# A fused fp32 transformer chain on one core: the two x halves of the FFN gate and up products in one 512-column matmul

## The reference, cut to what matters

```python
def swiglu(h, w_gate, w_up, w_down):                 # layers 0 and 1
    return (jax.nn.silu(h @ w_gate) * (h @ w_up)) @ w_down

def conv_ffn(x, g, w_up, dw_w, dw_b, w_down):        # layer 2
    h = causal_depthwise_conv(rms_norm_2(x, g) @ w_up, dw_w, dw_b)   # 3 taps over the tokens
    gate, up = h[..., :D_FF_2], h[..., D_FF_2:]
    return (jax.nn.silu(gate) * up) @ w_down
```

## Time and profile before

| | |
|---|---|
| time before, median of 3 runs | 981.87 us (979.51 to 983.39) |
| the profiled execution's own time | 980.03 us |
| its span (first to last instruction) | 978.3 us |
| PE busy | 934.4 us, 96% |
| PEld busy | 852.5 us, 87% |
| DVE busy | 535.2 us, 55% |
| ACT busy | 475.8 us, 49% |
| POOL busy | 336.8 us, 34% |
| mean granted TensorE clock | 0.984 of full |

### The profile page before, as it was taken

One profiled execution on the slowest core, in us unless ns is written; L12 is line 12 of the kernel. 1 busy time (PEld: TensorE's weight loads), 2 busy tenths in 40 slices (PEclk: granted clock), 3 DMA queues, 4 the chain that ended last, 5 costly groups with the idle time before them and its releaser, 6 DMA issues.

```text
span 978.3 us, 16764 instructions
## 1 busy us (share of the span) xinstructions
PE 934.4 (96%) x6404; PEld 852.5 (87%) x6404; DVE 535.2 (55%) x882; ACT 475.8 (49%) x767; POOL 336.8 (34%) x188
## 2 busy tenths in 40 slices
PE   4999999999999999999999999898999989999996
PEld 4899999999977899999999999586798789999995
DVE  3874444335455574444445595665565575666655
ACT  4753444434554574344444442467444465555542
POOL 1364433340000064444333279700100154444441
PEclk9999999999999999999999999798999999999999
DMA  9686666532431767666644665201443476566601
GB/s 302 199 251 200 193 193 188 179 116 80 160 117 45 213 200 235 178 186 193 193 151 130 174 155 185 87 1 44 130 172 86 151 222 192 178 182 193 193 22 44
DMA packets 187406, 154.35 MB, mean 158 GB/s; under 512 B 6573, under 2 KB 172685, under 8 KB 187357
## 3 DMA queue, kind: packets, MB, share of 16 engines
q1 hardware_dynamic: 184941, 148.67, 49.9%
q0 software_dynamic: 752, 2.39, 1.0%
q10 hardware_dynamic: 1664, 2.60, 0.8%
HBM read 152.04 MB, written 1.05 MB: 156 GB/s over the span
## 4 chain that ended last, share of the span: by engine, by line
PE 86%; DVE 5%; ACT 4%; POOL 2%; issue 1%; DMA 1%; SPq 0%; DVEq 0%; ACTq 0%
PE bank L1620 25%; PE bank L1622 25%; PE bank L1621 25%; PE bank L1712 2%; DMA raw<-in_pool_w 1%; DVE wl L964 1%; PE bank L2038 1%; PE bank L1637 1%; ACT wh L555 1%; PE bank L2110 1%; PE bank L1932 1%; PE bank L2187 1%; POOL st L1511 1%; PE bank L1931 1%; PE bank L2166 1%
## 5 line engine op out<-in xcount | busy, mean ns | idle before, releaser
L1531 POOL TENSOR_TENSOR dl<-draw,dh 128x1024 fp32r<-128x1024 f32 x66 | 239.4, 3630 | 292.8 <-ACT dh L599 292.7
L1620 PE MATMUL bank<-xh,wh 128*128 128x256 f32 x1192 | 338.8, 284 | 1.3 <-DVE xl L1182 0.7
L1622 PE MATMUL bank<-xh,wl 128*128 128x256 f32 x1192 | 338.1, 284 | 0.0
L1621 PE MATMUL bank<-xl,wh 128*128 128x256 f32 x1192 | 338.0, 284 | 0.0
L1620 PEld LDWEIGHTS bank<-xh,wh 128*128 128x128 f32 x1192 | 228.2, 191 | 5.4 <-DVE wl L964 1.2
L1621 PEld LDWEIGHTS bank<-xl,wh 128*128 128x128 f32 x1192 | 228.1, 191 | 3.0
L1622 PEld LDWEIGHTS bank<-xh,wl 128*128 128x128 f32 x1192 | 228.3, 192 | 0.3
L964 DVE TENSOR_TENSOR wl<-raw,wh 128x2048 fp32r<-128x2048 f32 (+5 forms) x53 | 112.5, 2129 | 57.6 <-ACT wh L555 57.6
L1064 DVE TENSOR_TENSOR wl<-raw,wh 128x2048 fp32r<-128x2048 f32 x57 | 137.4, 2410 | 1.4 <-ACT wh L622 1.4
L622 ACT ACTIVATE wh<-raw 128x2048 fp32r<-128x2048 f32 x57 | 108.7, 1906 | 6.4 <-DMA raw<-in_ffn_w_up 6.4
L1620 PE MATMUL bank<-dh,hh 128*128 128x512 f32 x264 | 105.1, 398 | 3.3 <-DVE hl L1070 3.3
(11 more groups left out here) (299 smaller groups left out, 1439.0 us busy)
## 6 DMA issues: line engine op xcount, KB each, us to landing
raw<-in_ffn_w_up SPq DMA_DIRECT2D x88, 512.0 KB, 6.1
draw<-in_ffn_w_down SPq DMA_DIRECT2D x66, 512.0 KB, 3.5
raw<-in_ffn_w_gate SPq DMA_DIRECT2D x44, 512.0 KB, 5.3
raw<-in_w_in SPq DMA_DIRECT2D x18, 512.0 KB, 5.1
raw<-in_xattn_wk SPq DMA_DIRECT2D x8, 512.0 KB, 4.6
raw<-in_mla_w_o SPq DMA_DIRECT2D x8, 512.0 KB, 4.0
raw<-in_xattn_wv SPq DMA_DIRECT2D x8, 512.0 KB, 4.3
raw<-in_w_out SPq DMA_DIRECT2D x8, 512.0 KB, 4.4
```

What stands on the lines that cost most here:

```text
L1531: pool.tensor_tensor(dl[s][:, :], draw[s][:, :], dh[s][:, :].bitcast(F32), ALU.subtract) \
L1620: pe.matmul(outp, a_hi, b_hi, start=start, stop=False, **kw)
L1621: pe.matmul(outp, a_hi, b_lo, start=False, stop=False, **kw)
L1622: return pe.matmul(outp, a_lo, b_hi, start=False, stop=stop, **kw)
```

## The change

**PE.** `xh` and `xl` become the two halves of one tile `xhl`. In `up`, each weight slice is used by one 512-column matmul, wh x (xh, xl), whose two 256-column results go to the left and right half of a bank, and by one 256-column matmul, wl x xh, which is added to the left half. Gate has a bank of its own, up another; even steps use banks 4 and 5, odd ones 6 and 7. The semaphore `gate_done` tells when the gate half of a step is done, `block_used` the end of the step, as before. `first_up` does step 0 in the old 256-column products, into the new places.

**DVE.** The two halves of a bank are added by a `tensor_reduce` of two elements, 512 values in and 256 out, to a tile in SBUF: `gs` for the gate, `us` for up. The low part of a slice (`weights_before`, slice j + 2) is made between the two additions, no longer at the end of the step before. All that follows (in ffn2 the taps) reads `gs` and `us` in SBUF instead of the bank.

**ACT.** Tanh (or the start of the gate's convolution) waits for `gs` only; `cu` waits for `us`. In ffn2 the tanh now stands ahead of the copy to `wh`. Loops have six steps instead of three. SP and POOL have no line changed.

The diff, without the lines that only rename or count:

```diff
-        xh = sb("xh", [P, KD, SEQ], F32R)
-        xl = sb("xl", [P, KD, SEQ], F32R)
+        xhl = sb("xhl", [P, 2, KD, SEQ], F32R)
+        xh, xl = xhl[:, 0, :, :], xhl[:, 1, :, :]
...
+        gs = at_("gs", [P, SEQ])
+        us = at_("us", [P, SEQ])
... ACT, step
+                    act.wait_ge(gate_sum, m + 1)
+                    if layer < 2:
+                        act.activation(th[s][:, :], gs[:, :], ACT.Tanh, scale=0.5).then_inc(tanh_done, 1)
+                    else:
+                        conv_start(0, gs, cg[s])
+                        act.wait_ge(up_sum, m + 1)
+                        conv_start(1, us, cu[s])
+                        act.wait_ge(conv_tap, 4 * (j + 1) - 2)
+                        act.activation(th[s][:, :], cg[s][:, :], ACT.Tanh, scale=0.5).then_inc(tanh_done, 1)
                     act.wait_ge(block_used, n + 1)
... DVE, step
+                    dve.wait_ge(gate_done, m + 1)
+                    dve.tensor_reduce(gs[:, :], pair[0][:, :].rearrange("p (a s) -> p s a", a=2), AX.X, ALU.add) \
+                       .then_inc(gate_sum, 1)
+                    if jj > 0:
+                        weights_before(j, i, jj)
+                    dve.wait_ge(gate_sum, m + 1)
+                    dve.wait_ge(block_used, n + 1)
+                    dve.tensor_reduce(us[:, :], pair[1][:, :].rearrange("p (a s) -> p s a", a=2), AX.X, ALU.add) \
+                       .then_inc(up_sum, 1)
+                    dve.wait_ge(up_sum, m + 1)
+                    g, u = gs[:, :], us[:, :]
                     if layer == 2:
+                        taps(0, gs, cg[s])
+                        taps(1, us, cu[s])
...
+                def weights_before(j, i, jj):
+                    if i is not None or jj + 2 < STEPS:
+                        ns = (n0 + jj - 1) % 3
+                        dve.wait_ge(hi_done, n0 + j + 3)
+                        dve.tensor_tensor(wl[ns][:, :], raw[ns][:, :], wh[ns][:, :].bitcast(F32),
+                                          ALU.subtract).then_inc(lo_done, 1)
+                    else:
+                        lo(n0 + jj + 2)
... PE, up
                     for half in range(2):
+                        b = bank[4 + 2 * (jj % 2) + half]
                         for k in range(KD):
                             a = (2 * k + half) * P
-                            ins = three(bank[4 + s][:, half * SEQ:(half + 1) * SEQ], wh[ns][:, a:a + P],
-                                        wl[ns][:, a:a + P], xh[:, k, :], xl[:, k, :], k == 0, k == KD - 1)
-                    ins.then_inc(block_used, 1)
+                            pe.matmul(b[:, :].rearrange("p (a s) -> p a s", a=2), wh[ns][:, a:a + P], xhl[:, :, k, :],
+                                      start=k == 0, stop=False, skip_group_check=True)
+                            ins = pe.matmul(b[:, 0:SEQ], wl[ns][:, a:a + P], xh[:, k, :], start=False,
+                                            stop=k == KD - 1, skip_group_check=True)
+                        ins.then_inc((gate_done, block_used)[half], 1)
```

More of the change, by code:

```diff
@@ L647, in ffn @@
                 step(0, None, 0)
-                with act.Fori(0, LOOPED // 3) as i:
-                    for s in range(1, 4):
-                        step(3 * i + s, i, s)
+                with act.Fori(0, LOOPED // 6) as i:
+                    for s in range(1, 7):
+                        step(6 * i + s, i, s)
                 for j in range(LOOPED + 1, STEPS):
@@ L1036, in step @@
                     n, m = n0 + j, m0 + j
-                    g, u = bank[4 + s][:, 0:SEQ], bank[4 + s][:, SEQ:2 * SEQ]
-                    if layer == 2:
[L1040 to L1049, removed]
+                    pair = bank[4 + 2 * (jj % 2)], bank[5 + 2 * (jj % 2)]
@@ new lines, in taps @@
+                    def taps(half, src, dst):
+                        dve.wait_ge(conv_in, 2 * j + half + 1)
+                        for back in (1, 2):
+                            if back == 2:
+                                dve.wait_ge(conv_tap, 4 * j + 2 * half + 1)
+                            c = C_DW + (2 - back) * NF2 + half * STEPS
+                            dve.scalar_tensor_tensor(
+                                out=dst[:, back:SEQ], in0=src[:, 0:SEQ - back],
+                                scalar=col[:, bass.ds(j + c, 1)], in1=dst[:, back:SEQ],
+                                op0=ALU.mult, op1=ALU.add).then_inc(conv_tap, 1)
@@ L1058, in step @@
                                              op0=ALU.mult, op1=ALU.mult).then_inc(prod_done, 1)
[L1060 to L1067, removed]
                     dve.wait_ge(h_hi, m + 1)
@@ L1073, in step @@
                         after(before)
-                    next_weights()
+                def weights_before(j, i, jj):
[6 more added lines that the diff above has]
+                        lo(n0 + jj + 2)
                 step(0, None, 0)
-                with dve.Fori(0, LOOPED // 3) as i:
-                    for s in range(1, 4):
-                        step(3 * i + s, i, s)
+                with dve.Fori(0, LOOPED // 6) as i:
+                    for s in range(1, 7):
+                        step(6 * i + s, i, s)
                 for j in range(LOOPED + 1, STEPS):
                     step(j, None, j)
+                lo(n0 + STEPS + 2)
             def after(name):
                 lo(at[name] + 3)
-            dve.sem_inc(prod_done, 3)
+            dve.sem_inc(prod_done, 2)
             dve.wait_ge(pos_loaded, 16)
@@ L1719, in ffn, with first_up @@
                     pe.wait_ge(cols_done, 2)
+                pe.wait_ge(mem_out, (1, 4, 8)[layer])
+                def first_up():
+                    pe.wait_ge(lo_done, n0 + 1)
+                    for of_lo in (False, True):
+                        for k in range(KD):
+                            pe.wait_ge(t_lo if of_lo else t_hi, KD * e + k + 1)
+                            for half in range(2):
+                                o = bank[4 + half][:, of_lo * SEQ:(of_lo + 1) * SEQ]
+                                a = (2 * k + half) * P
+                                for w_ in ((wh,) if of_lo else (wh, wl)):
+                                    ins = pe.matmul(o, w_[n0 % 3][:, a:a + P], (xl if of_lo else xh)[:, k, :],
+                                                    start=not of_lo and k == 0 and w_ is wh, stop=True,
+                                                    skip_group_check=True)
+                                if of_lo and k == KD - 1:
+                                    ins.then_inc((gate_done, block_used)[half], 1)
                 def up(j, jj):
                     n, m = n0 + j, m0 + j
-                    ns, s = (n0 + jj) % 3, (m0 + jj) % 3
+                    ns = (n0 + jj) % 3
                     pe.wait_ge(lo_done, n + 1)
@@ L1768, in ffn @@
                 pe.wait_ge(prod_done, m0 + 1)
-                first_product(n0, 4 + m0 % 3, e)
-                for j in range(1, 4):
+                first_up()
+                for j in range(1, 7):
                     up(j, j)
                     down(j - 1, j - 1, j == 1)
[L1774 to L1777, removed]
+                with pe.Fori(1, LOOPED // 6) as i:
+                    for s in range(1, 7):
+                        up(6 * i + s, s)
+                        down(6 * i + s - 1, s - 1)
                 up(LOOPED + 1, LOOPED + 1)
```

26 lines of the change are left out of this document (10 added, 16 removed).

## The result

The kernel after the change takes 999.15 us (median of 4 runs, 994.58 to 1002.54), the kernel before 982.63 us beside it (4 runs, 979.51 to 984.15). The ratio is 1.0189 with an interval of 1.0148 to 1.023: slower by 1.9%. The forecast was 1006.8 us, in a range of 976 to 1016.

The account below looks back on a forecast made before the run. It took PE to bound the kernel before (96% busy) and DVE to bound ffn2 afterwards. 980.03 plus 24.9 for ffn2 and 0 for ffn0 and ffn1 gave 1005, with 1.84 to the median 1006.8 us; range 976 to 1016.

Parts of the forecast that it names:

- The mechanism: ffn2: taps reading SBUF exclude POOL's `dl`, so DVE becomes the bound, with steps of 9.3 to 10.05 us; chance 0.71.
- The rival of free taps: ffn2: taps in SBUF are not held up, DVE's step is 7.7 us and PE stays the bound, 979 us; chance 0.17.
- the second: Rival on DVE: the additions cost twice, 1.3 us each, giving 1025 us; chance 0.08.
- the third: Rival on PE: a 512-column product from two places costs 2 x 120 ns, giving 1012 us; chance 0.04.
- PE's part: Up products of all FFNs: each of 1008 slices saves 6 to 11 ns, taken as 8 us in all.
- The estimate of 2.5 us: Up products on PE: by the skill's gap formula a slice saves 2.5 ns, the change 2.5 us; set aside for the rows.
- the DVE step of ffn2: Time from one `hl` end to the next in ffn2: 9.7 us, longer than PE's 8.43 us.
- the race of `wl` and `dl`: ffn2: both ready within 0.03 us; 9.3 us a step with `wl` first, 10.05 us with `dl` first.
- The sum for ffn2: `hl` of step 1 at 803.3, 18 steps of 9.7, last two 7.1 and 5.5: ends at 990.5, +24.9 us.
- The starts of ffn0 and ffn1: down(1) waits 1.4 or about 2.4 us in each; gain 5.4, loss 2.8 to 8 us, put at 0.
- the middle order: ffn2: 9.7 us a step, taken between the 9.3 us of `wl` first and the 10.05 us of `dl` first.
- `wl` always first: ffn2: low end of the main forecast, where `wl` precedes `dl` in every step at 9.3 us: 999.6 us.

Follow-up runs that it names:

- Experiment 2: Changed kernel, but the four taps of ffn2 read the bank instead of `gs` and `us`, leaving out part of the result: 980.39 us, one run.
- experiment 1: Changed kernel, but POOL's `dl` is a 64-column subtraction and a memset, leaving out the low part of the down weights: 977.85 us, one run.
- experiment 3: Changed kernel, but in ffn2 POOL makes the `dl` subtraction twice, once into an unused tile: 1034.16 us, one run.
- Experiment 4: Changed kernel, but in ffn2 `wl` is made at the end of the step again, with the additions kept: 985.86 us, ratio 1.0048 to the kernel before.
- experiment 6: Changed kernel, but `xh` and `xl` of a slice lie side by side in SBUF instead of in two places: 1001.87 us, one run.
- experiment 5: Changed kernel, but with ffn2 as before the change, so only ffn0 and ffn1 are changed: 981.17 us, ratio 0.9993 to the kernel before.
- experiment 7: Changed kernel, but ACT copies a bank's right half to SBUF, DVE adds it into the left half, and taps read the bank: 1002.63 us, ratio 1.0218.
- experiment 8: Changed kernel, but halves summed in the bank by ACT copy and DVE addition, gate copy ahead of `dh`, step 0 summed by PE: 974.80 us, ratio 0.9922.

## Why the prediction was right, and where its sizes were off

**The mechanism held.** DVE became the bound of ffn2 because the taps, reading SBUF, stand still while `dl` is at work. Experiment 2 moves the taps out of it and experiment 1 POOL, and either takes the steps back to 8.44 us; experiment 3 doubles POOL's part and adds 1.9 us. Experiment 4 shows the other half of it: with `wl` moved, the same taps and the same `dl` fit under PE's step. The rival of free taps, which had 0.17, is out: the first tap took 1.56 us (I had said over 2). Of the second, an addition takes 0.69 us and not 1.3. Of the third, experiment 6 shows that the two places cost nothing.

**PE's part** was 8 ns for a slice. Rows before and after: (5750 - 5640) / 16 is 6.9 ns, between the two bounds, 6 and 11. In other FFNs of the experiments the same up product takes 5.55 us, which is 12.5 ns a slice and above the bound (last section). The estimate of 2.5 us by the Trainium skill's gap (TensorE: Matmul & The Clock Gate, Back-to-back issue gap), which the page gives for an isolated matmul, is not borne out: 0.11 us in each of 63 steps is 6.9 us.

**The step that was mis-sized is the DVE step of ffn2.** I called the race of `wl` and `dl` a tie and took the middle, 9.7 us. It is not a toss for each step: in this trace and in that of experiment 6 the same 0.05 us decides it the same way in every step but the loop boundary, where 0.2 us more on DVE tip it the other way. The mean from `hl` of step 1 to that of step 19 is (967.82 - 803.99) / 18 = 9.10 us. It is made of 15 steps with `wl` first, two with `dl` first and the last one, 8.66 us:
- With `wl` first, 9.00 us and not 9.3. `dl` ends 2.25 us after `wl` (880.26 to 882.51), not 2.36, and the tap is through its own 0.48 us at 882.80, so it got going at 882.32 already, before the profile has `dl` end.
- With `dl` first, 10.12 us, which I had as 10.05. It came twice in the 18 steps.

I had also said that PE would wait at each down product of ffn2, some 18 times. It waited 15 times, at down(1) and then from down(7) on. Before that its steps took 8.44 to 8.59 us, which is no gain: DVE's took 9.0 there too, but PE was behind. After its wait of 4.88 us PE ran at the lower clock level (0.50 of full), down(1) took 809.82 - 804.57 = 5.25 us instead of 2.8, and down(2) came 11.0 us after it, 2 us more than DVE needs. PE ate this up at 0.56 us a step. So the late clock cost nothing where DVE sets the pace.

The stretch of ffn2's start (the clock is the first number behind the five engines):

```profile
804.00:809.60 5.60, 5.03 (x12) 4.00 (x13) 5.34 (x5) 2.11 (x3) 4.46 (x1) 0.50 0.70 196
```

Timeline of PE there, first matmul of down(1) and of the next up product:

```profile
804.57 0.77 PE L1640 MATMUL bank<-dh,hh 128*128 128x512 f32 x1 [4.88 <-DVE hl L1080]
...
809.82 0.59 PE L1768 MATMUL bank<-xhl,wh 128*128 128x512 f32 x1
```

**The sum for ffn2.** `hl` of steps 1, 19, 20 and 21 after, DVE:

```profile
803.99 0.43 DVE L1080 TENSOR_TENSOR hl<-pr,hh 128x256 fp32r<-128x256 f32 x1 [0.65 <-ACT hh L640]
...
967.82 0.42 DVE L1080 TENSOR_TENSOR hl<-pr,hh 128x256 fp32r<-128x256 f32 x1 [0.53 <-ACT hh L640]
...
974.39 0.42 DVE L1080 TENSOR_TENSOR hl<-pr,hh 128x256 fp32r<-128x256 f32 x1 [0.53 <-ACT hh L640]
...
979.55 0.42 DVE L1080 TENSOR_TENSOR hl<-pr,hh 128x256 fp32r<-128x256 f32 x1 [0.53 <-ACT hh L640]
```

A slip in my sum first: four additions at 0.61 us are 2.4 us and not 2.6; the 803.3 follows from 2.4. ffn2 starts 2.50 us later in this trace than in the one before (down(0) at 790.29 against 787.79), which I take off. `hl` of step 1 ends at 804.42, so at 801.9 where I had 803.3 (1.4 less). The 18 steps take 163.8 us where I had 174.6 (10.8 less), steps 20 and 21 6.57 and 5.16 where I had 7.1 and 5.5 (0.9 less). 24.9 - 13.1 is 11.8 us, which is what ffn2 lost.

**The starts of ffn0 and ffn1.** I had waits of 1.4 or, with a `dl` in between, 2.4 us. They were 2.47 and 1.76 us:

```profile
66.30 0.76 PE L1640 MATMUL bank<-dh,hh 128*128 128x512 f32 x1 [2.47 <-DVE hl L1080]
...
367.20 0.47 PE L1640 MATMUL bank<-dh,hh 128*128 128x512 f32 x1 [1.76 <-DVE hl L1080]
```

In ffn0 a slow step followed, as I had allowed for: the granted clock was 0.66 behind the wait, and the step took 9.91 us instead of 8.44. In experiment 2 the same wait of 2.48 us was followed by a clock of 1.00 and a step of 8.42. The stretch behind the wait, in the changed kernel and in experiment 2:

```profile
66.30:71.00 4.70, 4.70 (x14) 3.75 (x15) 4.67 (x4) 2.67 (x3) 4.29 (x1) 0.66 1.04 299
66.50:71.00 4.50, 4.50 (x22) 3.74 (x23) 4.46 (x4) 2.68 (x3) 4.08 (x1) 1.00 0.96 289
```

The two FFNs together came out at +2.5 us in the profiled execution, where I had 0; over ten runs experiment 5 shows no difference clear of noise. That the start waits come from `dl` too, and not from the additions alone, is shown by experiment 1, where they are gone.

**The total.** The profiled execution is 14.6 us above that of before (994.58 against 980.03). The medians are 16.5 apart, since the one is 4.6 us under its median and the other 2.6. The forecast of +24.9 was 10.3 above the 14.6 of the profiled execution: 13.1 too much in ffn2, 7.2 of them for the middle order, and 2.5 too little in ffn0 and ffn1 (0.3 us are left over). With `wl` always first my own sum gave 999.6, beside a median of 999.15. That it is so close is luck: it still has some 6 us too much in ffn2, against the 2.5 us of ffn0 and ffn1 and 2.7 us by which the profiled execution lies further under its median than the 1.84 that I used.

## What to carry to other kernels

An operation that moves from one memory to another changes not only its own length but whom it excludes: when a DVE instruction gets both operands from SBUF, look for POOL instructions beside it that read SBUF before adding busy times (here the subtraction `dl`; in experiment 1 a memset beside `wl` held nobody up). Where two engines race in a repeated step and the steps follow the pace of one of them, a few hundredths of a microsecond can decide the race the same way each time (16 of 18 steps here, all 18 in experiment 7; but 13 of 18 in experiment 2, where DVE did not set the pace). Forecast each outcome with a chance of its own rather than their mean, and in the code make the order certain (experiment 8 against 7). When a step is reordered, follow what it releases on other engines as well.

## What the runs showed of the hardware that I had not expected

**PE has two spacings for the same code.** A step is 8.44 or 8.34 us for a whole stretch, at a granted clock of 1.00 either way. It changes at a wait or a step behind it, or in the first steps of an FFN (in experiment 1, ffn1, the first step takes 8.36 us and the rest 8.44, without a wait). In experiment 2, ffn2, first matmuls of five downs running, one of which had to wait 0.23 us:

```profile
888.30 0.40 PE L1640 MATMUL bank<-dh,hh 128*128 128x512 f32 x1
...
896.75 0.40 PE L1640 MATMUL bank<-dh,hh 128*128 128x512 f32 x1
...
905.58 0.47 PE L1640 MATMUL bank<-dh,hh 128*128 128x512 f32 x1 [0.23 <-DVE hl L1080]
...
914.00 0.39 PE L1640 MATMUL bank<-dh,hh 128*128 128x512 f32 x1
922.34 0.39 PE L1640 MATMUL bank<-dh,hh 128*128 128x512 f32 x1
```

8.45 us ahead of the wait, 8.34 behind it (922.34 - 914.00). Which one an FFN gets differs between kernels whose code for that FFN is the same or nearly so: 8.34 in ffn0 and 8.44 in ffn1 in experiments 5 and 7, 8.44 and 8.34 in experiment 3. It is worth some 2 us in an FFN. The kernel before shows one spacing only, 8.55 us. What decides it stays open.

**The stage between the FFNs varies more than the gain.** The same 25 us in layer 2's mixer, whose code is unchanged, in the changed kernel (stretches, columns as above):

```profile
610.00:635.00 25.00, 23.60 (x99) 15.83 (x98) 16.90 (x46) 11.90 (x31) 21.22 (x21) 0.75 0.25 85
```

and in experiment 6:

```profile
610.00:635.00 25.00, 20.93 (x65) 13.10 (x63) 12.32 (x32) 9.27 (x23) 21.30 (x21) 0.56 0.25 84
```

The granted clock is 0.75 in the one and 0.56 in the other, and from ffn1 to ffn2 it takes 265.3 and 272.7 us. Between ffn0 and ffn1 it is 131.4 to 131.6 us in eight of the ten profiles and 135.3 in experiments 4 and 5, at a mean granted clock of 0.96 where the others have 1.00. Whether the clock makes the whole difference is not shown. A kernel run once can't be judged to better than that by its total, but can be by its steps.
